# A chunked recurrence with each head on its own 64 rows, its preparation moved among the transitions, and the modulation rows moved behind the substitution

## The reference

```python
def step(s, inp):
    r_t, w_t, k_t, v_t, kk_t, a_t = inp
    sa = jnp.einsum('bhvk,bhk->bhv', s, -kk_t)
    s = s * w_t[:, :, None, :] + sa[..., None] * (kk_t * a_t)[:, :, None, :] + v_t[..., None] * k_t[:, :, None, :]
    return s, (jnp.einsum('bhvk,bhk->bhv', s, r_t) if with_output else None)
...
yn = ((y - mean) * lax.rsqrt(var + RW_GN_EPS)).reshape(b_, n, RW_DIM) * ln_w + ln_b
bonus = jnp.einsum('blhn,bldhn,hn->blh', q['r'], q['k'], p['rw_rk'])[..., None] * q['v']
return (yn + bonus.reshape(b_, n, RW_DIM)) * q['g']
```

## Time and profile before

| | |
|---|---|
| median of 3 runs | 4474.1 us (4459.36, 4474.1, 4499.28) |
| the profiled execution | 4479.68 us |
| its span | 4477.9 us |
| mean granted clock | 0.874 |
| PE busy | 3615.5 us (81%), 21300 instructions |
| PE weight loads | 2181.8 us (49%) |
| DVE busy | 1630.9 us (36%) |
| ACT busy | 812.8 us (18%) |

### The profile page before, as it was taken

How to read it: one execution, slowest core, us unless ns; L and a number is a source line. 1 busy time by engine, 2 the same in 40 slices (tenths; PEclk the granted TensorE clock), 3 DMA queues, 4 the chain that set the end, 5 groups by cost and what they waited for, 6 DMA issues and landing times. The chain is left out here.

```text
span 4477.9 us, 51174 instructions
## 1 busy us (share of the span) xinstructions
PE 3615.5 (81%) x21300; PEld 2181.8 (49%) x21300; DVE 1630.9 (36%) x3319; ACT 812.8 (18%) x1565; POOL 52.1 (1%) x72
## 2 busy tenths in 40 slices
PE   5788988888887988869993878876887978848994
PEld 2466665656655555444443322233444444437883
DVE  2466556656346566450004100013223142241112
ACT  1333443333112112110001000001212121100101
POOL 0000000000000000000000000000000000000000
PEclk7889899988588989989995899987998989858997
DMA  3111112221101000031105899933010110037884
GB/s 127 44 58 61 34 49 67 67 67 52 52 38 57 28 28 28 29 150 38 66 38 198 362 428 428 428 122 112 38 40 37 40 77 0 38 125 278 331 327 155
DMA packets 98000, 530.74 MB, mean 119 GB/s; under 512 B 33569, under 2 KB 36113, under 8 KB 72993
## 3 DMA queue, kind: packets, MB, share of 16 engines
q1 hardware_dynamic: 90912, 503.06, 29.0%
q0 software_dynamic: 4608, 16.78, 1.0%
q10 hardware_dynamic: 2304, 8.39, 0.5%
HBM read 500.85 MB, written 27.34 MB: 118 GB/s over the span
## 5 line engine op out<-in xcount | busy, mean ns | idle before, releaser
L1902 PE MATMUL ex_ps<-ex_ring,ex_xs 128*64 128x512 f32 x1024 | 248.1, 642 | 61.8 <-DMA ex_ring<-expert_slabs_in 58.7
L569 PE MATMUL rw_ps<-hT,rw_w 128*128 128x512 f32 (+1 forms) x640 | 272.7, 556 | 0.4 <-DVE rw_kk L1051 0.4
L2639 PEld LDWEIGHTS ge_ps<-ge_xeT,ge_ring 128*128 128x128 f32 x2048 | 232.7, 193 | 10.5 <-issue 10.5
L2639 PE MATMUL ge_ps<-ge_xeT,ge_ring 128*128 128x128 f32 x2048 | 232.9, 276 | 2.9 <-DVE ge_xeT L2697 2.9
L2136 PE MATMUL mh_ps<-mh_w,xmT 128*128 128x512 f32 x512 | 221.5, 593 | 8.6 <-ACT mh_sg L2159 8.6
L1287 PE MATMUL sg_ps<-hTp,sg_w 128*128 128x512 f32 x384 | 179.5, 623 | 28.1 <-PEq L61 28.1
L1902 PEld LDWEIGHTS ex_ps<-ex_ring,ex_xs 128*64 128x64 f32 x1024 | 88.1, 147 | 221.2 <-issue 221.2
L2136 PEld LDWEIGHTS mh_ps<-mh_w,xmT 128*128 128x128 f32 x512 | 97.0, 190 | 132.5 <-issue 120.5
L569 PEld LDWEIGHTS rw_ps<-hT,rw_w 128*128 128x128 f32 x640 | 115.5, 198 | 70.5 <-issue 57.6
L2127 PE MATMUL mh_ps<-xmT,mh_w_ahead 128*128 128x512 f32 x256 | 121.0, 636 | 22.4 <-PEq L61 22.4
L1287 PEld LDWEIGHTS sg_ps<-hTp,sg_w 128*128 128x128 f32 x384 | 76.6, 201 | 117.6 <-issue 116.6
(11 more groups left out here) (568 smaller groups left out, 5760.6 us busy)
## 6 DMA issues: line engine op xcount, KB each, us to landing
ex_ring<-expert_slabs_in SPq DMA_DIRECT2D x96, 2048.0 KB, 19.8
ge_ring<-expert_slabs_in SPq DMA_DIRECT2D x48, 2048.0 KB, 12.6
rw_mod_w<-mod_w_in SPq DMA_DIRECT2D x64, 384.0 KB, 4.2
rw_mod_w<-ada_in SPq DMA_DIRECT2D x64, 256.0 KB, 3.3
mh_w_ahead<-head_slabs_in SPq DMA_DIRECT2D x8, 2048.0 KB, 10.3
mh_w<-head_slabs_in SPq DMA_DIRECT2D x8, 2048.0 KB, 10.3
rw_w<-rw_slabs_in SPq DMA_DIRECT2D x8, 1536.0 KB, 8.4
sg_w<-xbc_slabs_in SPq DMA_DIRECT2D x4, 3072.0 KB, 10.1
```

What stands on the lines that cost most here:

```text
L569: mm = pe.matmul(where[j, part], w[:, k, P * j:P * j + P], tokens, start=k == 0, stop=k == KC - 1)
L1902: mm = pe.matmul(ps[halves[j], bank, :], src[:, k, halves[j]], ring[:, (n + j) % RING, k, :], start=k == 0, stop=k == KC - 1)
L2639: mm = pe.matmul(ps[:, 2 + 2 * (j % 2) + n, P * f:P * f + P], w[:, k, P * f:P * f + P], xeT[:, j, k, :], start=k == 0, stop=k == KC - 1)
```

## The change

Each head's small products now have as input and output its own 64 partitions. `tk[:, u, side, :]` is now indexed by side: side 1 the values, side 0 the substitution, and heads lie on the partition halves. `keys` makes its products in two parts, 128 wide in bank 4 and, outside the context, 64 wide in bank 5, and has 16 products with `fold` where it had four transposes. `wu` writes both heads into one bank. `new_part` and the local output of `scan_step` become two accumulating products of 64 rows. ACT's and DVE's copies are of 128 partitions and half as many. The order of all engines is changed; modulate's bank is 1.

```diff
-        SCAN, Y, MOD, GATE, YT = (7, 0), 4, 6, 5, 7
+        SCAN, Y, MOD, GATE, YT = (7, 0), 4, 1, 5, 4
+        PRODUCTS = (0, 1, 3, 5, 6, 8, 10)
...
                     sp.wait_ge(s.mod_done, c + 1)
                     for row, _, out in mod_parts(c):
                         sp.dma_start(out, row).then_inc(s.mod_stored, 16)
+                    if c + 1 < PAIRS:
+                        mod_bias(c + 1)
+                    if c + 2 < PAIRS:
+                        next_pair(c + 2)
                     sp.wait_ge(s.readout, c + 1)
...
                 def turn_v(c):
-                    if c:
-                        pe.wait_ge(s.readout, c)
-                    for h in range(2):
-                        for x in range(RW_NCH):
-                            mm = pe.matmul(ps[64:P, 4 + 2 * h + x // 8, cols(x % 8)], vc[rows(h), cols(x)], fold[rows(h), :], start=True, stop=True)
+                    for x in range(RW_NCH):
+                        for h in range(2):
+                            mm = pe.matmul(ps[rows(h), 6 + x // 8, cols(x % 8)], vc[rows(h), cols(x)], fold[rows(h), :], start=True, stop=True)
+                    mm.then_inc(s.v_turned, 1)
...
                 def keys(c, q):
+                    if q == 0:
+                        pe.wait_ge(s.v_kept, 2 * c + 2)
+                        pe.wait_ge(s.readout, c)
+                    else:
+                        pe.wait_ge(s.masked, 10 * c + PRODUCTS[q])
+                    for x in range(4):
+                        for h in range(2):
+                            u = 4 * q + x
+                            mm = pe.matmul(ps[rows(h), 4, P * x:P * x + n], bk[rows(h), u, 64:P], kr[rows(h), u, 0:n], start=True, stop=True)
+                    mm.then_inc(s.products, 1)
+                    if not is_ctx(q):
                         for x in range(4):
-                            mm = pe.matmul(ps[:, 4 + h, P * x:P * x + n], bk[rows(h), u, :], kr[rows(h), u, 0:n], start=True, stop=True)
+                            for h in range(2):
+                                u = 4 * q + x
+                                mm = pe.matmul(ps[rows(h), 5, cols(x)], bk[rows(h), u, 0:64], kr[rows(h), u, 64:P], start=True, stop=True)
                         mm.then_inc(s.products, 1)
-                    for x in range(4):
-                        pe.transpose(ps[:, 6, P * x:P * x + P], bk[:, 4 * q + x, :], ident)
+                    for side in range(2):
+                        for x in range(4):
+                            for h in range(2):
+                                pe.matmul(ps[rows(h), 6, cols(2 * x + side)], bk[rows(h), 4 * q + x, cols(side)], fold[rows(h), :], start=True, stop=True)
...
                 def join_first(c):
-                    pe.wait_ge(s.turned, 2 * c + 2)
+                    pe.wait_ge(s.turned, 2 * c + 1)
...
                 def wu(c, q):
+                    if q >= 2:
+                        pe.wait_ge(s.wu_kept, 6 * c + q - 1)
+                    for x in range(4):
+                        for h in range(2):
                             u = 4 * q + x
-                            mm = pe.matmul(ps[0:64, 4 + h, P * x:P * x + P], xt[rows(h), u, :], kx[rows(h), u, :], start=True, stop=True)
+                            mm = pe.matmul(ps[rows(h), 4 + q % 2, P * x:P * x + P], xt[rows(h), u, :], kx[rows(h), u, :], start=True, stop=True)
...
                 def new_part(c):
-                            for h in range(2):
-                                mm = pe.matmul(ps[rows(h), 4 + g, cols(u % 8)], tk[:, u, h, P:192], tk[:, u, h, 64:P], start=True, stop=True)
+                            for side in range(2):
+                                for h in range(2):
+                                    mm = pe.matmul(ps[rows(h), 4 + g, cols(u % 8)], tk[rows(h), u, side, P:192], tk[rows(h), u, side, 64:P], start=side == 0, stop=side == 1)
```

The others, cut to their order:

```diff
@@ scalar
-                        keep_near(c, 0)
-                        keep_near(c, 1)
+                        keep_diag(c, 0)
                         if c:
                             deviation(c - 1)
-                        keep_near(c, 2)
+                        keep_diag(c, 1)
+                        keep_diag(c, 2)
...
+                        for d in range(2):
+                            act.copy(tk[:, of_dir(d), 1, 64:P], turned).then_inc(s.v_kept, 1)
+                        for g in range(3):
+                            keep_mid(c, g)
+                        keep_tokens(c, 0)
...
                     if core:
                         keep_wu(c, 1)
-                        keep_wu(c, 2)
...
+                        keep_wu(c, 2)
+                    if prep:
+                        centre(p, 0, 0, rc[:, :], ps[:, 2, :])
+                        factors(p, 0)
+                    if core:
                         for q in range(3, 6):
                             keep_wu(c, q)
@@ vector
                         exponents(p, 0)
+                    if core:
+                        dve.wait_ge(s.mod_bias, NMOD * (c + 1))
+                        dve.wait_ge(s.mod_used, KC * (c + 1))
+                        dve.tensor_tensor(mrow[:, :], ps[:, MOD, 0:MW], mrow[:, :], ALU.add).then_inc(s.mod_done, 1)
...
-                        for q in range(1, 5):
-                            keep_mr(c, q)
+                        keep_mr(c, 1)
+                        keep_mr(c, 2)
                     if prep:
+                        neighbours(p, 0, 0, rc[:, :], ps[:, 2, :], SEQ)
+                        dve.sem_inc(s.shifted_r, 1)
...
+                        write_keys(p, 0)
+                    if core:
+                        keep_mr(c, 3)
+                    if prep:
+                        fill(p, 0)
+                    if core:
+                        keep_mr(c, 4)
+                    if prep:
+                        exponents(p, 1)
                     if core:
                         keep_mr(c, 5)
...
                         scan_step(c, 1)
                         scan_step(c, 2)
                     if prep:
                         write_keys(p, 1)
                     if core:
-                        for step in range(6, 8):
+                        for step in range(3, 6):
                             scan_step(c, step)
```

208 lines of the change are left out of this document (93 added, 115 removed).

## The result

The kernel after takes 4324.6 us (median of four runs, 4318.4 to 4327.7), the kernel before, run beside it, 4468.7 (4459.4 to 4499.3). The ratio is 0.9669, 95% interval 0.9631 to 0.9707: 144 us faster, where 67 had been forecast and the range ended at 4370. The profiled execution of after took 4327.7 us, 151.9 less than that of before, and the windows place all of it in the recurrence.

A forecast was written before the change was run, and what follows sets the result against it. PE was taken to bound the pair, then its waits, then the clock. Seven pairs -38, clock -12, last pair -18 and prologue +1 made -67 us: 4407 beside the median, range 4370 to 4468.

The forecast's parts named there:

- Boundary: Start of a pair: turn_y no longer waits, 2.4 us of wait comes before keys, turn_v takes 1.6 instead of 2.76.
- Prices: PE work: own-row products at 0.067 us (64 columns) and 0.125 (128), new_part 6.4; net -1.0 us a pair.
- Idle: PE idle in the quick pair: 11.0 us against 15.1, at keys, value_part, new_part's end, scan and before near.
- rival B: Transitions: DVE becomes the bound, 3.5 us a pair, and no clock is won: 4444 us; chance 20%.
- Prologue: Before the pairs: projection before lora waits for a larger load, +1 us.
- The clock: Three slow pairs and the first: 35 us in all if the clock is lifted, else 0; a third taken, -12.
- The last pair: Final pair with readout: -12.5 us with terms partly at half clock, -27 all at full; -18 taken.
- A: Recurrence stage: the clock stays up through most of it, -99 us, 4375 us; chance 15%.
- C: New_part to near: the clock falls to 1.2 GHz, 13 us a pair slower, 4516 us; chance 9%.
- D: Own-row products: row halves share the bank's port, 0.115 instead of 0.067, +27 us a pair, 4626 us; chance 2%.
- E: wu and keys: wu's products stay at 0.18 us, keys' too, +4.4 us a pair, 4438 us; chance 4%.

The follow-up runs named there:

- experiment 12: Changed kernel with v's last latent projection parts ahead of the mr and n copy waits, turn_v behind turn_y, gate product behind the scan: 4293.7 us, ratio 0.9594.
- experiment 5: Changed kernel with DVE's preparation (r's neighbours, write_keys(0), fill(0), exponents(1)) back between the scan steps: 4365.4 us, ratio 0.9754.
- experiment 9: The changed kernel again, unchanged, in one batch with three later runs: 4326.0 us, ratio 0.9666 to the kernel before.
- the order alone: New order of all engines, old layout of products, copies and masks, turn_v still behind turn_y: 4425.1 us, ratio 0.9908 to the kernel before.
- the layout alone, experiment 2: New layout (own-row products, accumulating new_part and local output) with every call and copy in the old order: 4415.3 us, ratio 0.9876 to the kernel before.
- experiment 6: Changed kernel with the last two parts of v's latent projection ahead of the waits for the mr and n copies: 4319.2 us, ratio 0.9648.
- experiment 7: Experiment 6's kernel with the fold products of keys(0) also ahead of the wait for readout: 4307.7 us, ratio 0.9621.
- experiment 8: Changed kernel with turn_v behind turn_y instead of ahead of bonus: 4316.7 us, ratio 0.9643.
- experiment 10: Experiment 7's kernel with the gate product behind the scan instead of ahead of it: 4297.6 us, ratio 0.9603.
- experiment 3: Changed kernel with the loop over heads outside in keys, value_part, wu, mr and new_part: 4454.7 us, ratio 0.9963.
- experiment 11: Experiment 10's kernel with the gate product done three times, same result in the same bank: 4293.5 us, ratio 0.9592.

## Why the prediction was wrong, step by step

**Direction and waits right, the clock mis-sized, and the sum under half.** By its own steps for the seven pairs and the rest:

- *Boundary.* Right: turn_y's wait gone, one of 2.4 before keys(0) (2.52), turn_v 1.6 (1.5). The old stretch from near to turn_v's end is 16.2 us (316.40 to 332.6); less 4.25 of waits and 1.1 of turn_v, plus 2.4, the steps make 13.2, and 10.65 were measured. The difference is the clock: the earlier trace rows have this stretch at 0.75, and the sum had carried its durations over.
- *Prices.* The own-row products cost 0.058 us with 64 columns and 0.115 with 128, not 0.067 and 0.125; new_part 5.8 instead of 6.4. The 0.067 had been read from one half of near in the earlier trace rows, 1.6 us, in which the clock fell (it is low from 838.0 us on); at a clock of 1.00 it takes 1.44 (517.85 to 519.29 in experiment 12). Net work was put at -1.0 a pair and came to -2 to -3 (704 to 696 against 717 in seven). This term was mis-sized by 6 to 15 us in all.
- *Idle.* 11.0 forecast, 9.7 measured in the second pair: keys(0) 2.4 (2.5), value_part 0.6 (0.4), ahead of the gate 2.5 (1.8), scan 2.5 (2.1), before near 3.0 (2.9). This part stands. So do its statements that DVE has no stall before the first mask and modulate no wait for DMA. That the stall's end gives nothing in itself was not tested. That DVE's preparation fits among the transitions (the ground against rival B) after shows itself, with 1.8 us of wait behind them; experiment 5 shows what it costs elsewhere.
- *Prologue.* +1, measured -1.7, and +0.4 in the profile of experiment 9: within its scatter.
- **The clock, the step that failed.** "In all" was put at 35 us: the excess of the slow pairs over the quick and 7 of the first, and a third of that taken. But the quick pair was not free of it: a mean of 0.91 over 899.5 us is 81 us. The 46 us left out are what quick and slow pairs share, 6.3 us in the second pair: the boundary's 0.75 and the transitions' 0.91 of the earlier trace rows, as part of "PE busy 110.4", which the sum took for work. The chip gave back 57 of the 81. The reading of the slow pairs was also partial. It named value_part and the joins as what went before the fall; in two of the three the longest low stretch begins in turn_y's wait of 4.5 us and goes on for 18 us of full work, and only in the fifth pair does it stand in the transitions, behind no wait over 1.1 us:

```profile
450.93 1.97 PE L614 MATMUL rw_ps<-consts,rw_tk 64*64 64x64 f32 x32 [4.51 <-DVE rw_tk L1119]
```

```profile
448.90:469.30 20.40, 17.95 (x95) 11.15 (x96) 7.58 (x19) 9.36 (x17) 0.00 (x0) 0.50 0.29 83
773.10:797.00 23.90, 23.72 (x164) 19.31 (x162) 2.50 (x7) 10.40 (x17) 0.00 (x0) 0.50 0.00 1
```

- **The last pair** went by -36.8, not -18. Its terms were worked out at half clock (-12.5) and at full (-27); the clock rose from 0.61 to 0.85, which is 36 us of lost time less (48.7 to 13.2), and idle time fell by 4. Same step, same error: the half clock of the earlier trace rows was taken for a property of the products. Either half of the change lifts it by itself: from this near to the next stage's first product it is 131.7 us before and 95.3 after, 104.7 with the order alone (clock 0.76) and 113.1 with the layout alone (0.85).

By numbers: clock -57 for -12, last pair -37 for -18, work -22 for -7, idle -34 for -29 (the forecast had rounded these two up to -38), start -2 for +1: -152 for -67, and 64 of the 85 between them in the first two.

**The rivals.** A (the clock stays up, 4375) was the true case, and too small for the same reason: it gave back 35 of the 81. B is out: the wait behind the transitions is 1.8 us, and the clock was won. C, the clock falling in the scan, did not happen: 1.00 from new_part to near. But the next boundary pays, 1.7 us in near and turn_v (0.84) and 1.7 behind keys(0), which experiments 6 to 8 and 10 to 12 move about. D, that two row halves can't use one bank at a time, is refuted by more than near: 192 records of new_part in 5.81 us write three banks, one after the other, from both halves at 0.060 us a product, and experiment 3, with the same banks and one head after the other, is the dearer. E is out: wu at 1.09.

**What makes the clock.** Three explanations of the gain stood against each other. That alternating heads hold it: not needed, by experiment 3. That new layout or new order holds it by itself: each leaves 51 or 78 of the 81. That it follows PE's waits: shown for the boundary by experiments 7, 8 and 10 to 12, with the exceptions in the table; there 2 us of useless work in the hole took the low stretch out of near in every pair. For the rest of the pair it is not shown, and that is the larger part: of before's 79 us (this count uses the unrounded clock) 44 are lost in the first 30 us of each pair and 36 behind them, of after's 23 all in the first 30. Behind them the order alone still loses 27 and the layout alone 21, so it took both. That the layout alone, with more waits than before, loses less to the clock speaks against waits as the whole cause. The Trainium skill, "TensorE: Matmul & The Clock Gate", section "HAM oscillation — how this bites in real kernels", describes a loop with short groups of products, in which the wait for the next transfer sends TensorE back to the half clock in every iteration, and advises to restructure the loop so that it stays at full. In this trace the waits at the boundary are for DVE and ACT, and the low stretches behind them come back in every pair (7 of 7 in after) and leave with them. For those 36 us (joins and transitions) and for the last pair it stays open what raised the clock.

## What to carry over

Work out the time lost to the clock of the whole stretch first, length times one minus the granted clock, of the quick iterations too, and ask what wait precedes each low stretch: at the boundary here, taking that wait away returned the clock as well. Durations read at a low clock are not prices. Moves that take work out of a stretch belong together with those that fill it: the same modulates cost 6.7 us more a pair in a scan without projections than between the keys. A fixed hole in PE's order, here the wait before near, is the place for work that can stand anywhere: the gate product there gave about 10 us (4307.7 to 4297.6, in two batches). And look at all boundaries of a run before reading one: in experiment 10 three of the seven look unlike the one shown.

## What the runs showed of the hardware

- Two row halves of TensorE in alternation take fp32 products of 64 rows at 0.058 us (64 columns) and 0.115 us (128 columns) from start to start, writing the same bank; the same products of keys, value_part, wu, mr and new_part head after head cost 125 us more PE time in seven pairs, some 12 of it clock (experiment 3).
- Useless products in an idle stretch can leave a kernel no slower: 16 extra products of 1 us or so, 4293.5 against 4297.6 us (experiment 11).
- A wait of PE of 2.4 to 2.9 us for another engine was followed by a stretch at half clock in 50 of 52 cases, at the boundaries of after and experiments 6 to 8, 10 and 11. A wait of 1.8 us before near was in 4 of 14 (experiments 10 and 12), and the 1.8 us ahead of the gate in none of after's seven.
- The amount of waiting alone doesn't set the clock: the layout alone is idle 110 us and loses 51 to the clock, before is idle 101 and loses 81 (experiment 2).
- With all pairs at the full clock they are equal to 0.02 us (107.63 to 107.64, experiment 12); in experiments 6 and 10, with the clock low at changing places, they scatter over 1.2 to 1.7 us, and in after, where it is low at the same places in each, over 0.15.
